# Differential attention's q, k and V by token halves from high and low parts, and three masks of the top-256 search summed on ScalarE

## The chip, the cores and the metric

The kernel runs on one core of a Trainium2 chip. Times are device microseconds (us) of that core from start to end of the program. TensorE is called PE here, VectorE DVE, ScalarE ACT, GpSimd POOL and SyncE SP; PS is PSUM, TensorE's accumulator memory.

## The reference, cut to what matters

```python
S, D, TOPK, Q_BLOCK = 1024, 1024, 256, 128
h = x @ w_in                                    # fp32; columns: a_u a_v b_q b_k b_v c_q c_k c_v i_q i_k i_w
# differential attention: 4 heads, q and k of 2 x 64, v of 128
p = softmax(b_q @ b_k.T / 8 - slope[h] * abs(qpos - kpos)); attn = p[0] - lam * p[1]
out_b = rms_norm(attn @ b_v)
# sparse attention: each query keeps its 256 best keys
score = sum_h i_w[h] * relu(i_q[h] @ i_k.T);  sel = top_k(score, 256)    # block-causal mask
out_c = softmax over sel of c_q @ c_k.T, times c_v
# gMLP mixer
v = layer_norm(gelu(a_v));  out_a = gelu(a_u) * (w_s @ v + b_s)
x = layer_norm(ALPHA * x + concat(out_a, out_b, out_c) @ w_out)          # then FFN, then a second layer
```

The change touches how `b_q`, `b_k` and `b_v` are computed, how the 256 best keys are found, and where the bias `-slope * distance` is made. Nothing after the first layer's attention changes in its own code but for names of semaphores.

## The kernel before

The first layer's input product is done in stages on PE, one weight chunk of 512 KB after another. SP loads the chunks into `ring`, which has four slots; a slot is loaded again once the chunk in it is used (`weights_used`). The order of the stages is the list `ORDER`; the class `Ledger` counts from it which slot, which pair of PSUM banks (four pairs) and which of the three `w_parts` buffers each chunk has. The stages around the change, in PE's order, are: `cqk` and `score` (interleaved), `auv` (gMLP's u and v), `turn_ws`, `bqk` (q and k of differential attention, 8 chunks), `bv` (its V, 4 chunks), `gmlp`, then differential attention itself with `ada` chunks as fill.

`by_feature` (L1296; its products are L1305) does `bqk`: a chunk is 128 output columns, and the product runs over both halves of the 1024 tokens, 16 products of 128x512, with inputs `xT` and `ring` read as plain fp32. `by_token` (L1308; products L1319) does `auv` and `bv`: a chunk is two of the eight 128-row tiles of the weights, for all eight token tiles. The trace records one such fp32 product of 128x512 as two instructions.

Later stages (from `out1` on) do a product in three passes instead. `split_weight` on POOL (L2839) makes of a chunk in `ring` a high part, rounded to fp32r (L2844), and the rest, the low part (L2847), in one of the `w_parts` buffers. The activations are split alike, and PE adds high·high, high·low and low·high. A `w_parts` buffer is free again when PE has used it (`parts_used`).

DVE meanwhile searches the 256th largest score of each query (lines 2250 to 2281). `score` holds the six query blocks 2 to 7, of 384 to 1024 keys. A round fixes one bit of the threshold, 32 rounds in all. In a round the blocks go in two groups of three; for each group two small instructions on three columns work out the next threshold (L2269, L2275), then three counts (L2256) compare a block with its threshold, write the mask as bf16 into `tested` and sum it into `enough`. After the last round come a tail (L2281 to L2298: for each block a mask of ties, a scan that ranks them and three passes that give `mask`), and then the layer norm of gMLP's v (L2307 to L2318), which ends with `v_normed`. PE's `gmlp` (L1477) waits for that. ACT copies results out of PSUM, and POOL has nothing to do while the search runs.

Of the kernel before, what the change touches and what calls it, by code (L numbers as in the profile page):

```python
# [56 lines left out]
def whole(n, dmas=1):  # L57
    return [(dmas, False)] * n
# [5 lines left out]

def sevens(n):
    return [(1, "seven")] * n
# [13 lines left out]

def down_steps(n_k):
    return [(1, "down")] * (7 * n_k)
# [10 lines left out]
    "bqk": (whole(4), [0, 1, 2, 3]),  # L93
    "bv": (whole(4), [None, None, None, 3]),
# [28 lines left out]
         ("bqk", 0), ("bqk", 1), ("bv", 0), ("gmlp", 0), ("ada", 0), ("turn_mix", 0), ("out1", 0), ("turn_mod", 0), ("out1", 1)]  # L123
# [21 lines left out]
class Ledger:  # L145


    def __init__(self):
# [6 lines left out]
        for stage, i in ORDER:  # L155
            chunks, units = STAGES[stage] if stage != "idx" else IDX[i]
            self.pairs_at[stage, i] = list(pairs)
            for c, (dmas, kind) in enumerate(chunks):
                s, q = n_loads % RING, n_halves // 2 % PARTS
# [16 lines left out]
                if kind:  # L176
# [5 lines left out]
                    n_halves += 2  # L182
# [51 lines left out]
def program(nc, t, out):  # L234
    L = Ledger()
    with ExitStack() as ctx:
# [32 lines left out]
        xT = view(0, KT, S)  # L269
# [21 lines left out]
        ranks = view(165.5, S)  # L291
# [7 lines left out]
        dist = view(165.5, S)  # L299
# [126 lines left out]
        dist_made = sem("dist_made")  # L426
        bias_made = sem("bias_made")
        lam_sums = sem("lam_sums")
        lam_exps = sem("lam_exps")
# [4 lines left out]
        norm_var = sem("norm_var")  # L434
        norm_sqrt = sem("norm_sqrt")
        score_added = sem("score_added")
        topk_step, topk_done = sem("topk_step"), sem("topk_done")
# [25 lines left out]
        fl_exp, fl_ln, cum_done = sem("fl_exp"), sem("fl_ln"), sem("cum_done")  # L463
        selw_made, counts_made = sem("selw_made"), sem("counts_made")
        cum_high, cum_split, causal_row_made = sem("cum_high"), sem("cum_split"), sem("causal_row_made")
        pool_w_loaded, pool_w_zeroed = sem("pool_w_loaded"), sem("pool_w_zeroed")
# [664 lines left out]
        def b_bias(u, m):  # L1131
            h, b = heads4[u]
            return bias8[:, h, P * (NB - 1 - b):S], bias_made, 4
# [40 lines left out]
        def after_c(act, u):  # L1174
            rows_c(act, u)
            if u == 4:
                act.wait_ge(norm_var, 2)
                act.activation(o_ssq[:, :], o_ssq[:, :], ACT.Sqrt).then_inc(norm_sqrt, 1)
# [117 lines left out]
        def by_feature(pe, stage, i, source):  # L1296

            for c in range(len(STAGES[stage][0])):
                s, p = L.slot(stage, i, c), L.pair(stage, i, c)
                w = ring[:, s, :].rearrange("p (k n) -> p k n", k=KT)  # L1300
                weights_here(pe, stage, i, c)
                pair_here(pe, stage, i, c)
                for h in HALVES:
                    for k in range(KT):
                        mm = pe.matmul(PS[:, 2 * p + h, :], w[:, k, :], source[:, k, half_of(h)],  # L1305
                                       start=(k == 0), stop=(k == KT - 1))
                mm.then_inc(weights_used[s], 1)

        def by_token(pe, stage, source, width=512):

            for c in range(4):
                s = L.slot(stage, 0, c)
                weights_here(pe, stage, 0, c)
                for k in (2 * c, 2 * c + 1):
                    for b in range(NB):
                        p = L.pair(stage, 0, b // 2)
                        if k == 0 and b % 2 == 0:
                            pair_here(pe, stage, 0, b // 2)
                        mm = pe.matmul(PS[:, 2 * p + b % 2, 0:width], source[:, k, tok(b)],  # L1319
                                       ring[:, s, (k % 2) * width:(k % 2 + 1) * width],  # L1320
                                       start=(k == 0), stop=(k == KT - 1))
                        if k == KT - 1 and b % 2 == 1 and b < NB - 1:
                            mm.then_inc(psum_full[p], 1)
                mm.then_inc(weights_used[s], 1)
# [65 lines left out]
        def _(pe):  # L1390
# [68 lines left out]
            by_token(pe, "auv", xT)  # L1459
# [1690 lines left out]
```

## Time and profile before

| what | value |
|---|---|
| time, median of 3 runs | 2914.8 us (2908.94 to 2917.13) |
| the profiled execution, its own time | 2907.3 us |
| its span | 2905.6 us |
| PE busy | 2804.6 us, 97% of the span |
| DVE, POOL, ACT busy | 1528.2, 1278.1 and 932.2 us |
| PE on the chain of work that ended last | 86% |

The span is the time from the first to the last instruction of the profile. "Busy" counts instructions that run; a DVE or POOL instruction that has been issued and waits inside the engine counts as busy too, so two records of the same form and different lengths tell of a wait. In a timeline, "x2" means two records of one form merged into one line, with the time from the first's start to the second's end.

### The profile page before, as it was taken

The page shows a single profiled execution, that of the slowest core. Times are in us where ns is not written, and L with a number is a line of the kernel's source. Part 1 is how long each engine was busy: PE and PEld are TensorE (multiplying, and loading weights), DVE is VectorE, ACT ScalarE, POOL GpSimd, SP SyncE. Part 2 cuts the span into 40 slices and gives each one's busy share as a digit, 9 for nine tenths or more (in the row PEclk, how much of TensorE's full clock was granted, in tenths as well). Part 3 has the DMA queues.
Part 4 walks back from the last instruction along what each step waited for, and adds up shares of the span by engine and source line. Part 5 has one row for each costly group of instructions (what it writes and reads, how often), then busy time and mean ns, then how long its engine had stood idle before and what let it go on. Part 6 is the DMA issues. An engine that isn't in the chain of part 4 may idle for free.

```text
span 2905.6 us, 33901 instructions
## 1 busy us (share of the span) xinstructions
PE 2804.6 (97%) x12861; PEld 2071.6 (71%) x12861; DVE 1528.2 (53%) x2414; ACT 932.2 (32%) x1590; POOL 1278.1 (44%) x848
## 2 busy tenths in 40 slices
PE   8999999889999999999999999988999899999998
PEld 5444457468888888887778888855466788888886
DVE  0599977656723334243652203556536722235998
ACT  2401036541233332112333200156103344444443
POOL 2000000036777776666677677700126587753020
PEclk9999999999999999999999999999999999999999
DMA  5111137233422223534433333200556333346854
GB/s 114 30 36 37 40 93 195 88 119 119 131 84 87 87 87 116 211 141 168 129 105 116 123 95 97 71 1 1 180 158 197 117 116 108 117 166 220 280 191 172
DMA packets 343393, 344.59 MB, mean 119 GB/s; under 512 B 18368, under 2 KB 261312, under 8 KB 343232
## 3 DMA queue, kind: packets, MB, share of 16 engines
q1 hardware_dynamic: 319424, 275.33, 30.7%
q10 hardware_dynamic: 21328, 59.97, 5.3%
q0 software_dynamic: 2480, 7.13, 1.0%
q8 instruction: 103, 1.69, 0.2%
q14 instruction: 58, 0.48, 0.0%
HBM read 284.61 MB, written 57.77 MB: 118 GB/s over the span
## 4 chain that ended last, share of the span: by engine, by line
PE 86%; DVE 7%; ACT 2%; issue 2%; DMA 1%; ACTq 0%; POOL 0%; SPq 0%; DVEq 0%; POOLq 0%
PE PS L535 25%; PE PS L1355 13%; PE PS L1367 11%; PE PS L851 9%; PE PS L1319 5%; PE PS L1305 4%; PE PS L1598 4%; PE PS L965 3%; PE PS L1436 2%; PE PS L983 2%; PE PS L1003 2%; PE PS L1547 1%; PE PS L1409 1%; PE PS L995 1%; PE PS L1450 1%
## 5 line engine op out<-in xcount | busy, mean ns | idle before, releaser
L2844 POOL TENSOR_SCALAR w_parts<-ring 128x1024 fp32r<-128x1024 f32 x166 | 205.5, 1238 | 802.3 <-DMA ring<-in_w_out 276.7
L594 DVE TENSOR_TENSOR arena<-arena,PS 128x512 f32<-128x512 f32 x266 | 182.9, 687 | 538.6 <-PE PS L535 537.3
L2847 POOL TENSOR_TENSOR w_parts<-ring,w_parts 128x1024 fp32r<-128x1024 f32 x166 | 445.3, 2682 | 13.8
L851 PE MATMUL PS<-w_parts,hid_high 128*128 128x512 f32 x896 | 276.4, 390 | 5.7 <-DVE w_parts L816 4.1
L535 PE MATMUL PS<-tx_high,w_parts 128*128 128x512 f32 x832 | 264.5, 389 | 0.0
L1355 PE MATMUL PS<-hT_high,w_parts 128*128 128x512 f32 x800 | 248.7, 391 | 7.9 <-DVE hT_low L2439 6.5
L1367 PE MATMUL PS<-w_parts,hid_high 128*128 128x512 f32 x704 | 218.3, 391 | 3.9 <-DVE hid_low L636 2.2
L573 POOL TENSOR_TENSOR w_parts<-arena,w_parts 128x512 fp32r<-128x512 f32 x152 | 194.4, 1291 | 44.6 <-ACT w_parts L554 44.5
L573 POOL TENSOR_TENSOR w_parts<-ring,w_parts 128x512 fp32r<-128x512 f32 x114 | 147.3, 1292 | 131.5 <-ACT w_parts L554 131.5
L851 PEld LDWEIGHTS PS<-w_parts,hid_high 128*128 128x128 f32 x896 | 167.7, 188 | 42.6 <-DVE w_parts L816 6.3
L1355 PEld LDWEIGHTS PS<-hT_high,w_parts 128*128 128x128 f32 x800 | 150.4, 188 | 41.1 <-DVE hT_low L2439 8.2
L535 PEld LDWEIGHTS PS<-tx_high,w_parts 128*128 128x128 f32 x832 | 156.2, 188 | 32.3
L851 PE MATMUL PS<-w_parts,hid_low 128*128 128x512 f32 x448 | 174.3, 389 | 0.0
L1073 DVE CUSTOM_DVE_ANT_0 arena<-PS,arena 128x1024 f32<-128x1024 f32 (+7 forms) x160 | 114.8, 755 | 110.7 <-PE PS L971 53.1
L2256 DVE TENSOR_SCALAR_CACHE_REDUCE arena<-arena,misc 128x384 bf16<-128x384 f32 (+2 forms) x192 | 171.4, 942 | 2.2
L535 PE MATMUL PS<-tx_low,w_parts 128*128 128x512 f32 x416 | 161.8, 389 | 0.0
L1355 PE MATMUL PS<-hT_low,w_parts 128*128 128x512 f32 x400 | 155.8, 389 | 0.0
L1367 PEld LDWEIGHTS PS<-w_parts,hid_high 128*128 128x128 f32 x704 | 132.7, 189 | 32.1 <-issue 4.7
L2907 POOL CAST arena<-ident 128x128 bf16<-128x128 f32 x1 | 0.3, 290 | 335.8 <-DVE arena L2298 335.8
L554 ACT CAST w_parts<-arena 128x512 fp32r<-128x512 f32 x152 | 93.7, 618 | 143.0 <-PE PS L535 120.7
L1319 PE MATMUL PS<-ring,arena 128*128 128x512 f32 (+1 forms) x384 | 138.8, 523 | 0.0
L535 PE MATMUL PS<-x1T_high,w_parts 128*128 128x512 f32 x432 | 138.8, 389 | 0.0
(358 smaller groups left out, 5827.6 us busy)
## 6 DMA issues: line engine op xcount, KB each, us to landing
ring<-in_w_in SPq DMA_DIRECT2D x96, 512.0 KB, 3.7
arena<-hid_spill SPq DMA_DIRECT2D x172, 256.0 KB, 3.7
hid_spill<-arena ACTq DMA_DIRECT2D x54, 512.0 KB, 2.9
ring<-in_w_gu SPq DMA_DIRECT2D x52, 512.0 KB, 3.9
ring<-in_w_ada SPq DMA_DIRECT2D x48, 512.0 KB, 5.3
ring<-in_w_ff SPq DMA_DIRECT2D x96, 256.0 KB, 2.9
ring<-in_w_down SPq DMA_DIRECT2D x44, 512.0 KB, 3.7
ring<-in_w_ff SPq DMA_DIRECT2D x40, 512.0 KB, 4.1
```

Source lines behind the costliest of these rows:

```text
L535: mm = pe.matmul(self.product(g, m), w[:, at], x[:, k, :], start=(k == 0 and i == 0), stop=(k == 3 and i == 2))
L573: pool.tensor_tensor(low, self.raw(n), high.bitcast(F32), ALU.subtract).then_inc(self.split_low, 1)
L594: dve.tensor_tensor(out, a, self.product(g, m), ALU.add).then_inc(self.combined, 1)
L851: mm = pe.matmul(PS[:, 4 * (p % 2) + u, :], x, w, start=(j == 0 and i == 0), stop=(j == self.n_k - 1 and i == 2))
L1305: mm = pe.matmul(PS[:, 2 * p + h, :], w[:, k, :], source[:, k, half_of(h)], start=(k == 0), stop=(k == KT - 1))
L1319: mm = pe.matmul(PS[:, 2 * p + b % 2, 0:width], source[:, k, tok(b)], ring[:, s, (k % 2) * width:(k % 2 + 1) * width], start=(k == 0), sto ...
L1355: mm = pe.matmul(PS[:, 2 * p + bank, :], w[:, q, k * P:(k + 1) * P], x[:, k, half_of(h)], start=(k == order[0] and n == 0), stop=(k == ord ...
L1367: mm = pe.matmul(PS[:, 2 * p + half, :], x[:, k, at], w[:, q, half_of(half)], start=(first and n == 0), stop=(last and n == 2))
L1598: mm = pe.matmul(PS[:, 2 * p + 1, :], w[:, k, :], x[:, half_of(h)], start=(k == ks[0]), stop=(k == ks[-1]))
L2256: stepped(dve.tensor_scalar(tested[b], score[b], threshold(column[b]), None, op, ALU.add, accum_out=enough[:, column[b]:column[b] + 1]))
L2844: pool.tensor_scalar(w_high[:, q, :], ring[:, s, :], 1.0, 1.0, ALU.mult, ALU.mult).then_inc(weights_high, 1)
L2847: pool.tensor_tensor(w_low[:, q, :], ring[:, s, :], w_high[:, q, :].bitcast(F32), ALU.subtract).then_inc(weights_used[s], 1)
```

## The change

1. `bqk` and `bv` are done in three passes from high and low parts, and by halves of the tokens. `in_features` and `in_tokens` take the place of `by_feature` and `by_token` there; the order is bqk, bv for tokens 0 to 511, then bqk, bv for tokens 512 to 1023. So each of the 12 chunks is loaded and split twice, 24 chunks of 24 products. Chunks of the new kind `"two"` alternate between the `w_parts` buffers 1 and 2. ACT rounds `xT` (`high_in`), POOL subtracts (`low_in`). For tokens 512 on, the high part is written over the low part of tokens 0 to 511, so that it waits for PE's use of each V chunk of the first half.
2. The search's masks of blocks 7, 6 and 5 (1024, 896, 768 keys) are made without a sum; ACT sums them, by a Square pass over `tested` with accumulation (`sum_masks`). The groups are now (7, 2, 3) and (6, 5, 4). DVE's threshold step of a group waits for ACT's sums of that group (`topk_summed`).
3. ACT's other work is put between the sums, at fixed rounds (`beside_bit`): it is in order, so a copy that waits for PE holds back the next sum, and PE gets a copy no sooner than the round it stands in.
4. In `auv` the last chunk goes token tile by token tile, so that the pairs of banks are full one after another.
5. The distance and bias of differential attention move from the start of the program (POOL, DVE) to behind the search (POOL, and four ACT copies with a scale).

```diff
-    "bqk": (whole(4), [0, 1, 2, 3]),
-    "bv": (whole(4), [None, None, None, 3]),
+    "bqk": (alternate(8), [1, 3, 5, 7]),
+    "bv": (alternate(4), [None, 3]),
...
+            for c in range(8):
+                p, q = L.pair("bqk", h, c // 2), L.part("bqk", h, c)
+                split_here(pe, "bqk", h, c)
+                if c % 2 == 0:
+                    pair_here(pe, "bqk", h, c // 2)
+                for k in range(KT):
+                    if c == 0:
+                        pe.wait_ge(xin_low, KT * h + k + 1)
...
+            def high_in(h, k):
+                for b in range(4 * h, 4 * h + 4) if k == 0 else ():
+                    freed(act, "turn_x", b // 4, b % 4)
+                if h == 1 and k % 2 == 0:
+                    q = L.part("bv", 0, k // 2)
+                    act.wait_ge(parts_used[q], L.part_uses("bv", 0, k // 2) + 1)
+                act.copy(xin(h)[0][:, k, half_of(1 - h)], xT[:, k, half_of(h)]).then_inc(xin_high, 1)
...
+            def beside_bit(i):
+                if i == 0:
+                    copy_cqk(0, 1)
+                if i == 2:
+                    copy_cqk(1, 0)
+                if i == 5:
+                    copy_cqk(1, 1)
+                    act.wait_ge(score_added, len(SCORE_UNITS))
+                if 6 <= i < 14:
+                    high_in(0, i - 6)
+                if 14 <= i < 18:
+                    copy_auv(i - 14)
+                if i == 17:
+                    copy_ws()
+                if i in (18, 20, 23, 25):
+                    copy_tiles("bqk", 0, (18, 20, 23, 25).index(i), bqkT)
+                if 25 <= i < 29:
+                    high_in(1, 2 * (i - 25))
+                    high_in(1, 2 * (i - 25) + 1)
+                if i == 28:
+                    copy_bv(0, 0)
+                    copy_bv(0, 1)
...
                 for b in groups[g]:
-                    stepped(dve.tensor_scalar(tested[b], score[b], threshold(column[b]), None, op, ALU.add,
-                                              accum_out=enough[:, column[b]:column[b] + 1]))
-                counted[g] = steps[0]
+                    if b in ACT_SUMS:
+                        dve.tensor_scalar(tested[b], score[b], threshold(column[b]), None, op).then_inc(topk_masked, 1)
+                        masks[0] += 1
+                    else:
+                        stepped(dve.tensor_scalar(tested[b], score[b], threshold(column[b]), None, op, ALU.add,
+                                                  accum_out=enough[:, column[b]:column[b] + 1]))
...
+            for c in range(2, 8):
+                split_weight("bqk", 0, c)
+            for c in range(3):
+                split_weight("bv", 0, c)
+            low_in(1, 0)
+            low_in(1, 1)
+            split_weight("bv", 0, 3)
```

DVE in a round of the search, before: L2269 and L2275 are the small steps, L2256 the counts.

```order
L2269 TENSOR_SCALAR misc<-misc 128x3
L2275 SCALAR_TENSOR_TENSOR misc<-misc 128x3
L2256 TENSOR_SCALAR arena,misc<-arena,misc 128x384
L2256 TENSOR_SCALAR arena,misc<-arena,misc 128x512
L2256 TENSOR_SCALAR arena,misc<-arena,misc 128x1024
L2269 TENSOR_SCALAR misc<-misc 128x3
L2275 SCALAR_TENSOR_TENSOR misc<-misc 128x3
L2256 TENSOR_SCALAR arena,misc<-arena,misc 128x640
L2256 TENSOR_SCALAR arena,misc<-arena,misc 128x768
L2256 TENSOR_SCALAR arena,misc<-arena,misc 128x896
```

The same round in the changed kernel: L2355 and L2361 are the small steps, L2338 the masks without a sum, L2341 the counts.

```order
L2355 TENSOR_SCALAR misc<-misc 128x3
L2361 SCALAR_TENSOR_TENSOR misc<-misc 128x3
L2338 TENSOR_SCALAR arena<-arena,misc 128x1024
L2341 TENSOR_SCALAR arena,misc<-arena,misc 128x384
L2341 TENSOR_SCALAR arena,misc<-arena,misc 128x512
L2355 TENSOR_SCALAR misc<-misc 128x3
L2361 SCALAR_TENSOR_TENSOR misc<-misc 128x3
L2338 TENSOR_SCALAR arena<-arena,misc 128x896
L2338 TENSOR_SCALAR arena<-arena,misc 128x768
L2341 TENSOR_SCALAR arena,misc<-arena,misc 128x640
```

Two counts have gone from the second group and one from the first; 1024 now stands ahead of its group.

POOL between its small loads at the start and its cast of `ident`, before: nothing stands between the load of `pool_w` and the cast (L2907), which waits for the search; the weights split behind it are those of `out1`.

```order
L2899 MEMSET arena 64x4x64
L2900 MEMSET pool_w 128x256
L2904 DMA pool_w<-in_w_pool 64x64 x4
L2907 CAST arena<-ident 128x128
L2844 TENSOR_SCALAR w_parts<-ring 128x1024
L2847 TENSOR_TENSOR w_parts<-ring,w_parts 128x1024
```

In the changed kernel 24 chunks are split there (L2932 high, L2935 low) and 16 pieces of the activations (L2993); this is the place from the first half's V on.

```order
L2935 TENSOR_TENSOR w_parts<-ring,w_parts 128x1024
L2932 TENSOR_SCALAR w_parts<-ring 128x1024
L2935 TENSOR_TENSOR w_parts<-ring,w_parts 128x1024
L2993 TENSOR_TENSOR xT_r<-xT,xT_r 128x512 x2
L2932 TENSOR_SCALAR w_parts<-ring 128x1024
L2935 TENSOR_TENSOR w_parts<-ring,w_parts 128x1024
L2993 TENSOR_TENSOR xT_r<-xT,xT_r 128x512 x2
L2932 TENSOR_SCALAR w_parts<-ring 128x1024
L2935 TENSOR_TENSOR w_parts<-ring,w_parts 128x1024
L2993 TENSOR_TENSOR xT_r<-xT,xT_r 128x512 x2
L2932 TENSOR_SCALAR w_parts<-ring 128x1024
L2935 TENSOR_TENSOR w_parts<-ring,w_parts 128x1024
```

The last chunk of the first half's V now stands behind the first two pieces of the second half's activations.

ACT between gMLP's copies and the norm's square root, before: one copy of the weights turned (L1779), eight copies of `bqk` (L1663).

```order
L1779 COPY wsT<-PS 128x512
L1663 COPY arena<-PS 128x1024 x8
L1783 ACT_TABLE_LOAD
L1783 ACTIVATE arena<-arena 128x32
L1787 COPY arena<-PS 128x1024 x4
L1790 COPY arena<-misc 128x256
```

In the changed kernel, from the round of index 25 on: L1707 copies `bqk`, L1838 is `high_in`, L1811 the sums.

```order
L1044 ACTIVATE arena,misc<-arena,misc 128x1024 x2
L1303 COPY arena<-PS 128x512
L1305 DMA ada_rows_spill<-arena 4x512
L1058 COPY arena<-PS 128x512
L1044 ACTIVATE arena,misc<-arena,misc 128x128 x2
L1058 COPY arena<-PS 128x512 x2
L1044 ACTIVATE arena,misc<-arena,misc 128x896 x2
L1058 COPY arena<-PS 128x128
L1044 ACTIVATE arena,misc<-arena,misc 128x256 x2
L1303 COPY arena<-PS 128x512
L1305 DMA ada_rows_spill<-arena 4x512
L1058 COPY arena<-PS 128x512
```

Each pair of L1838 now stands behind three sums of a round of the search.

## Rows read from the trace of the kernel before

**Rows 1.** Windows: busy us (instructions) per engine, PEclk, DMA share, GB/s.
```profile
150.80:346.60 195.80, 195.80 (x461) 86.93 (x460) 191.34 (x521) 16.12 (x20) 0.00 (x0) 1.00 0.13 38
```

**Rows 2.** Chain of work in order of time: start us, us, what.
```profile
237.18 109.87 PE PS L1305 x256
347.05 54.93 PE PS L1319 x128
401.98 3.43 PE PS L1477 x8
```

**Rows 3.** Timeline of DVE: search begins, one round, its tail begins (start us, us).
```profile
150.31 0.48 DVE L2242 MEMSET arena<- 64x64 f32 x6
...
161.69 0.16 DVE L2269 TENSOR_SCALAR misc<-misc 128x3 int32<-128x3 f32 x1
161.88 0.16 DVE L2275 SCALAR_TENSOR_TENSOR misc<-misc 128x3 int32<-128x3 int32 x1
...
163.29 1.27 DVE L2256 TENSOR_SCALAR_CACHE_REDUCE arena<-arena,misc 128x1024 bf16<-128x1024 f32 x1
...
167.69 0.17 DVE L2269 TENSOR_SCALAR misc<-misc 128x3 int32<-128x3 f32 x1
...
347.80 0.17 DVE L2281 TENSOR_SCALAR misc<-misc 128x6 f32<-128x6 f32 x1
```

**Rows 4.** Timeline of DVE, end of the search's tail and first norm step.
```profile
363.98 0.68 DVE L2286 TENSOR_SCALAR arena<-arena,misc 128x896 bf16<-128x896 f32 x1
...
369.67 0.75 DVE L2286 TENSOR_SCALAR arena<-arena,misc 128x1024 bf16<-128x1024 f32 x1
...
376.03 2.28 DVE L2307 TENSOR_REDUCE arena<-arena 128x32 f32<-128x2048 f32 x1
```

**Rows 5.** Timeline of DVE, last step of the gMLP norm.
```profile
391.05 2.29 DVE L2318 TENSOR_TENSOR arena<-arena 128x2048 f32<-128x2048 f32 x1
```

**Rows 6.** Chain of the whole span, a stage from high and low parts.
```profile
626.63 43.79 PE PS L1367 x192
```

**Rows 7.** Timeline of POOL in that stage: one weight chunk.
```profile
637.97 1.05 POOL L2844 TENSOR_SCALAR w_parts<-ring 128x1024 fp32r<-128x1024 f32 x1 [1.91 <-PE PS L1367]
639.10 2.38 POOL L2847 TENSOR_TENSOR w_parts<-ring,w_parts 128x1024 fp32r<-128x1024 f32 x1
```

**Rows 8.** One source line of POOL, 128x512: duration ns min/median/max.
```profile
L573 POOL TENSOR_TENSOR w_parts<-arena,w_parts x152: 1280/1288/1312, 808.7 to 2566.9; 128x512 fp32r<-128x512 f32 x152
```

**Rows 9.** Timeline of DVE around 1436 us, POOL splitting beside it.
```profile
1436.17 5.34 DVE L2397 TENSOR_TENSOR arena<-arena 128x1024 f32<-128x1024 f32 x2
1443.14 1.90 DVE L2480 TENSOR_SCALAR misc<-misc 128x4 f32<-128x4 f32 x1 [1.63 <-ACTq L1719]
```

**Rows 10.** Timeline of POOL in the same stretch.
```profile
1436.05 1.05 POOL L2844 TENSOR_SCALAR w_parts<-ring 128x1024 fp32r<-128x1024 f32 x1 [1.00 <-PE PS L1355]
1437.18 3.25 POOL L2847 TENSOR_TENSOR w_parts<-ring,w_parts 128x1024 fp32r<-128x1024 f32 x1
...
1442.62 2.39 POOL L2847 TENSOR_TENSOR w_parts<-ring,w_parts 128x1024 fp32r<-128x1024 f32 x1
```

**Rows 11.** Timeline of DVE around 1778 us.
```profile
1778.17 1.43 DVE L2640 TENSOR_SCALAR arena<-arena,misc 128x1024 f32<-128x1024 f32 x1
1779.63 4.62 DVE L2643 SCALAR_TENSOR_TENSOR arena<-arena,misc 128x1023 f32<-128x1023 f32 x2
```

**Rows 12.** Timeline of POOL in the same stretch.
```profile
1777.76 1.30 POOL L2844 TENSOR_SCALAR w_parts<-ring 128x1024 fp32r<-128x1024 f32 x1 [0.71 <-PE PS L1355]
1779.14 2.71 POOL L2847 TENSOR_TENSOR w_parts<-ring,w_parts 128x1024 fp32r<-128x1024 f32 x1
```

**Rows 13.** Timeline of ACT: a copy from PSUM, an accumulating pass.
```profile
250.95 1.01 ACT L1663 COPY arena<-PS 128x1024 f32<-128x1024 f32 x1 [12.61 <-PE PS L1305]
...
410.58 1.15 ACT L1033 ACTIVATE arena<-arena,misc 128x1024 f32<-128x1024 f32 x1 [5.95 <-DVE misc L1073]
```

**Rows 14.** DMA issues, from the page: KB each, median us from issue to landing.
```profile
ring<-in_w_in SPq DMA_DIRECT2D x96, 512.0 KB, 3.7
```

More of the change, by code:

```diff
@@ L1294, in rows_out, with by_token @@
             act.dma_start(ada_dram[:, 512 * g:512 * (g + 1)], ada_row[0:P:32, g % 2, :]).then_inc(ada_stored, 16)
[L1296 to L1309, printed above, removed]
+        def by_token(pe, stage, source, width=512, by_tile=False):
             for c in range(4):
@@ L1313, in by_token @@
                 weights_here(pe, stage, 0, c)
-                for k in (2 * c, 2 * c + 1):
[L1315 to L1322, printed above, removed]
+                steps = ([(k, b) for b in range(NB) for k in (2 * c, 2 * c + 1)] if by_tile and c == 3 else
+                         [(k, b) for k in (2 * c, 2 * c + 1) for b in range(NB)])
@@ new lines, in by_token @@
+                for k, b in steps:
+                    p = L.pair(stage, 0, b // 2)
+                    if k == 0 and b % 2 == 0:
+                        pair_here(pe, stage, 0, b // 2)
+                    mm = pe.matmul(PS[:, 2 * p + b % 2, 0:width], source[:, k, tok(b)],
+                                   ring[:, s, (k % 2) * width:(k % 2 + 1) * width],
+                                   start=(k == 0), stop=(k == KT - 1))
+                    if k == KT - 1 and b % 2 == 1 and b < NB - 1:
+                        mm.then_inc(psum_full[p], 1)
@@ new lines, in _ @@
+            for k in range(KT):
+                if k % 2 == 0 and k < 6:
+                    s = L.slot("auv", 0, k // 2)
+                    pool.wait_ge(weights_used[s], L.slot_uses("auv", 0, k // 2) + 1)
+                if k == 6:
+                    unit_here(pool, "auv", 0, 1)
+                low_in(0, k)
+            for c in range(2, 8):
+                split_weight("bqk", 0, c)
+            for c in range(3):
+                split_weight("bv", 0, c)
+            low_in(1, 0)
+            low_in(1, 1)
@@ new lines, in _ @@
+            split_weight("bv", 0, 3)
+            low_in(1, 2)
+            low_in(1, 3)
+            split_weight("bqk", 1, 0)
+            low_in(1, 4)
+            low_in(1, 5)
+            split_weight("bqk", 1, 1)
+            low_in(1, 6)
+            low_in(1, 7)
+            for c in range(2, 8):
+                split_weight("bqk", 1, c)
+            for c in range(4):
+                split_weight("bv", 1, c)
+            pool.wait_ge(topk_done, NB - 2)
+            pool.iota(dist, pattern=[[-1, S]], base=S - P, channel_multiplier=1,
+                      allow_small_or_imprecise_dtypes=True).then_inc(dist_made, 1)
@@ new lines, in _ @@
+            pool.iota(behind, pattern=[[1, P]], base=0, channel_multiplier=-1,
+                      allow_small_or_imprecise_dtypes=True).then_inc(dist_made, 1)
+            pool.wait_ge(dist_made, 2)
+            for part in (dist[:, S - P:S], behind):
+                pool.tensor_scalar(part, part, 0.0, None, ALU.max).then_inc(dist_made, 1)
+            pool.wait_ge(dist_made, 4)
+            pool.tensor_tensor(dist[:, S - P:S], dist[:, S - P:S], behind, ALU.add).then_inc(dist_made, 1)
+            for h in range(4):
+                pool.wait_ge(dist_made, 5 + h + 1)
+                pool.memset(bias8[0:64, h, S - 64:S], NEG).then_inc(bias_made, 1)
```

180 lines of the change are left out of this document (113 added, 67 removed).

## The prediction

> **What bounds the kernel now.** I read the windows first, then the chain of waits, then DVE's timeline, and last the places where POOL splits weights beside DVE. While the search runs, PE is busy for all of 195.8 us and DVE for 191.3, and POOL for nothing [rows 1]. The chain runs through PE alone: 109.87 us of `bqk`, 54.93 of `bv`, then `gmlp` at 401.98 [rows 2]. DVE ends its norm at 391.05 + 2.29 = 393.3 [rows 5]. So PE is the bound here and DVE has 8.7 us to spare. What PE gives up beyond that is gained only if DVE's chain (search, tail, norm) becomes shorter too. `gmlp` needs `v_normed`, and attention follows it; this stage is therefore settled by one number, the time at which `gmlp` can start, now 402.0.
>
> **PE's products.** Before: 109.87 + 54.93 = 164.8 us [rows 2]. After: 24 chunks of 24 passes, 576 of them. 192 such passes take 43.79 us [rows 6], so a chunk takes 5.47 and all take 131.4. PE alone would be 33.4 us shorter, and `gmlp` could start at 368.6.
>
> **DVE's rounds with nothing beside them.** A round is 167.69 - 161.69 = 6.00 us [rows 3]. The count of 1024 keys has a record of 1.27 us, of which about 0.07 lies under the next. A mask of the same form without a sum stands in the tail, 0.75 us for 1024 keys and 0.68 for 896 [rows 4], with a like overlap. So 1024 keys go from 1.20 to 0.67, and by the same slopes 896 from 1.07 to 0.60 and 768 from 0.93 to 0.53. That takes off 1.40 and a round is 4.6 us. The search took 347.7 - 150.8 = 197 [rows 3]; 33 passes over the blocks make it 46 us shorter. The tail to 376.0 is 28.3 us, the norm to 393.3 is 17.3 [rows 3 to 5]; neither changes.
>
> **ACT's sums.** An accumulating pass over 1024 elements is 1.15 us [rows 13]; with 896 and 768 in proportion about 3.1 us a round, under DVE's 4.6. A copy from PSUM beside it is 1.01 [rows 13], and a round still fits. ACT comes free for PE only in its fixed rounds, though: that is where delays of DVE reach PE.
>
> **POOL's splits, beside the search for the first time.** A chunk takes POOL 1.05 + 2.38 us and a gap of 0.08, 3.5 us of PE's 5.47 [rows 7], so POOL keeps pace if left alone. The 16 low passes over 128x512 are 1.29 each [rows 8]. What these do to DVE is the term that decides. At 1443.14 a DVE instruction on four columns takes 1.90 us and ends at 1445.04; POOL's subtraction beside it runs from 1442.62 to 1445.01 [rows 9, 10]. At 1778.17 a DVE pass with one SBUF input and no sum, the form of the masks, takes 1.43 us instead of 0.75 and ends 0.54 after POOL's pass (1777.76 + 1.30) [rows 11, 12]. POOL's next subtraction then takes 2.71 instead of 2.38, since it waits for that pass. Two DVE additions with two SBUF inputs, some 2.4 us of work, take 5.34 while POOL splits one chunk, and POOL's subtraction takes 3.25 [rows 9, 10]. I read this as one port that either engine holds for a whole instruction, and that goes to the other in between. It is met by DVE instructions with two SBUF inputs and by plain tensor-scalar ones.
>
> In a round these are the two small steps of each group and the three masks, seven instructions; the three counts left (some 2.0 us) can run beside POOL if they don't need the port. No row shows a count beside POOL. The form is slower for 1024 keys (1.27 against 0.75) [rows 3, 4], so I take it as free of the port; were it not, the result is in the fourth case below. The Trainium skill (SBUF — State Buffer, Who interferes with whom) says that a `tensor_scalar` which also writes out its accumulator does not enter the modes that take the shared ports. By that rule the counts are free and the sum stays; without it `gmlp` would be some 7 us later. No run shown here tells.
>
> **How a round goes beside splits.** Take DVE released by the end of a subtraction. Mask and counts last about 1.9 us, the two small steps 0.4. POOL's next rounding starts 1.9 us after the last subtraction's end (the idle time in [rows 7]), so DVE's second small step meets it and waits up to 1.0, and the mask behind it meets the subtraction and waits about 2.3. Then the same state is there again, one chunk later. So half a round costs one chunk, and a round 2 x 5.47 = 10.9 us instead of 4.6. It is the pattern of the two additions per chunk in [rows 9].
>
> **The stage walked through.**
> - `auv` is as long as `bv` (54.93) and ends with `turn_ws` at 237.18 [rows 2]; it begins at about 181.8, and its first of four chunks ends at 195.5. Only then can the first new chunk be loaded, which takes 3.7 us [rows 14]. So the rounds of index 0 to 8 pass at 4.6 (the last ends at 196).
> - From 199 to 240 POOL has two splits and eight low passes, 17 us on the port. I let DVE lose somewhat over half of it, 10 us: round 17 ends at 248 instead of 238. PE's first chunk needs a copy in round 15 and starts some 4 us late, at about 242.
> - Rounds 18 to 21 run beside splits at 10.9 each, to about 291.
> - POOL then stands, in order, before the first two low passes of the second half. These wait for ACT's `high_in` in round 25, and the split of the last V chunk is behind them. PE has used what was split by 242 + 11 x 5.47 = 302 and waits. Rounds 22 to 25 are undisturbed and end at about 312; ACT's pass, two low passes and a split put PE back at 321. PE loses 19 us.
> - The second half's last pieces stand in round 28, again beside splits, at about 339: PE loses some 11 us more. PE's end is then 321 + 13 x 5.47 + 11 = 403, about as before.
> - Rounds 29 to 31 end at about 365. In the tail nearly every instruction has two SBUF inputs or is a plain tensor-scalar one. Until POOL is done (398) two or three get through per chunk; I take 46 us instead of 28.3, to 411. The norm is undisturbed: 411.3 + 17.3 = 428.6.
>
> `gmlp` starts at 428.6 instead of 402.0, 26.6 us later. ACT's bv and bias copies (4 x some 1.0, after the square root at 421) and the table load end at about 429 and are hidden behind that wait; the moved iota and distance work of POOL (about 3 us from 411) lie there too. If DVE were on time they would end some 8 us behind PE, which is also when ACT's first exponential was due before (410.58 [rows 13] against `gmlp` at 401.98). Taking the bias from DVE's start gives nothing, as DVE idles there.
>
> **The sum.** The profiled execution took 2907.3 us. 2907.3 + 26.6 = 2933.9. The median of the runs shown is 7.5 us above it (2914.8), so I forecast 2941.4 us.
>
> **The rivals.**
> - *Port as above* (forecast): 2941, with 2930 to 2955 for the phase of the two engines. For it: the three places in [rows 9 to 12], one of them four columns wide, as the search's small steps nearly are. Against it: in all of them POOL and DVE met in other stages, never in the search.
> - *No meeting that matters* (the other side): masks that write bf16, or steps on three columns, slip past POOL. Then rounds stay at 4.6, ACT's copies wait for PE rather than the reverse, DVE's norm ends at about 350 to 363, and PE is the bound at 368.6 plus some 3.8 at the start of the second half, where ACT and POOL must follow PE's last V chunk: 372.4, 29.6 us earlier. 2914.8 - 29.6 = 2885. It decides where v_normed comes before 402; for that DVE may lose at most some 38 us to POOL, whose time on the port is 24 x 3.43 + 16 x 1.29 = 103 us. The tail and masks alone make that hard.
> - *Half of it*: either the masks or the small steps are free. A round beside splits is then some 7 to 8 us, round 31 ends at about 336, PE loses 8 to 10 us, the norm ends at 400 to 404. Time 2912 to 2917, no change.
> - *Counts too*: every DVE pass of a round takes the port. PE's first chunk is another 4 us late and the second half's start 3 more, v_normed at 436: 2949. With ACT's sums late as well it could reach 2965.
>
> **How the numbers follow.** Chances: port as above 0.62, counts too or worse 0.08, half of it 0.11, no meeting 0.19. The time is that of the first, 2941. The range runs from 2886 to 2962, so that it takes in the half case and the way between the cases, and leaves out most of the no-meeting case and the worst. The first case's own range is 2930 to 2955. About 0.3% (8.7 us) is what a measurement of this kernel can tell from no change. Faster by more: 0.19 and a little of the half case, 0.21. Within: 0.10. Slower by more: 0.69.
>
> **What would show it.** In the changed kernel's trace: (1) chunks of 24 passes at 5.47 us wherever PE doesn't wait; (2) rounds of 4.6 us before 199 us and of about 11 us from 248 to 290, with masks and small steps of 2 to 3 us and counts of unchanged length; (3) a wait of PE of some 19 us before the last V chunk of the first half; (4) a tail of about 46 us, and PE waiting for DVE before `gmlp` until about 429. Masks of 0.75 us beside splits would make the prediction wrong, as would `gmlp` before 402.

## The result, and the profile of the changed kernel

| | before | changed |
|---|---|---|
| time, median | 2912.8 us (4 runs, 2908.9 to 2917.1) | 2933.9 us (4 runs, 2932.9 to 2936.0) |
| profiled execution, its span | 2907.3, 2905.6 us | 2933.6, 2931.4 us |
| `gmlp` starts | 401.98 [rows 2] | 421.98 |
| attention's first product starts | 407.09 | 429.92 |

The ratio of the times is 1.0073 with an interval of 1.0055 to 1.0090, so the change makes the kernel slower. Of the 25.8 us by which the span grew, 22.8 stand at attention's first product.

Windows of the changed kernel, columns as in [rows 1]:

```profile
150.80:346.60 195.80, 171.61 (x545) 106.37 (x544) 191.48 (x413) 117.51 (x226) 75.09 (x47) 0.93 0.22 60
354.00:404.40 50.40, 46.16 (x204) 37.92 (x202) 49.28 (x34) 6.07 (x7) 28.41 (x15) 0.99 0.29 84
```

The first line is the stretch of [rows 1]. PE is no longer busy throughout (171.6 of 195.8 us), and DVE still is. DVE's busy time is the same as before although three sums a round are gone from it. POOL, idle before, is busy for 75.1 us. The second line holds the end of the search's last round and its tail. The tail's first instruction (L2368, on six columns) starts at 356.66 and the norm's first at 404.43, so the tail takes 47.8 us; before it took 28.2 [rows 3, 4].

What PE waits for between 230 and 425 us (instruction, what was waited for, us in total, times, longest):

```profile
PE PS L1516 <- issue: 21.8, 1, 21.8
PE PS L1358 <- POOL w_parts L2935: 11.8, 1, 11.8
PE PS L1339 <- POOL xT_r L2993: 7.6, 3, 6.1
PE PS L1339 <- issue: 3.1, 1, 3.1
PE PS L1339 <- POOL w_parts L2935: 1.1, 1, 1.1
```

L1516 is `gmlp`. It waits for 21.8 us; the profile names nobody for it, and the chain shows whom: it comes down DVE's search, tail (to 404.4) and norm. The others are, in this order, the last V chunk of the first half, the inputs of the second half's first chunk, the first chunk of all, and one more chunk. Without them PE would be done over 20 us earlier, and `gmlp` would start no sooner.

The wait of 11.8 us goes through ACT. In these rows of ACT, POOL and PE, ACT's rounding of the second half's inputs stands behind its sums and copies of a round, POOL's low passes wait for it, and the split that PE needs is behind them:

```profile
308.23 1.14 ACT L1838 CAST xT_r<-xT 128x512 fp32r<-128x512 f32 x2
...
308.92 2.48 POOL L2993 TENSOR_TENSOR xT_r<-xT,xT_r 128x512 fp32r<-128x512 f32 x2 [12.47 <-ACT xT_r L1838]
311.37 1.04 POOL L2932 TENSOR_SCALAR w_parts<-ring 128x1024 fp32r<-128x1024 f32 x1
312.49 2.59 POOL L2935 TENSOR_TENSOR w_parts<-ring,w_parts 128x1024 fp32r<-128x1024 f32 x1
...
315.14 0.80 PE L1358 MATMUL PS<-w_parts,bqkT_r 128*128 128x512 f32 x1 [11.77 <-POOL w_parts L2935]
```

The list of ACT's instructions given for the changed kernel in the section on the change (L1044, L1058, L1303) is not this place. Those are attention's, from about 433 us on.

The DVE instructions from 150 to 404 us by shape (busy us, mean ns of one). L2338 are the masks without a sum, L2341 the counts, L2355 and L2361 the small steps:

```profile
L2338 DVE TENSOR_SCALAR arena<-arena,misc 128x1024 bf16<-128x1024 f32 x32 | 37.4, 1168 | 1.1
L2338 DVE TENSOR_SCALAR arena<-arena,misc 128x768 bf16<-128x768 f32 x32 | 33.3, 1041 | 0.0
L2341 DVE TENSOR_SCALAR_CACHE_REDUCE arena<-arena,misc 128x640 bf16<-128x640 f32 x32 | 27.9, 872 | 0.0
L2355 DVE TENSOR_SCALAR misc<-misc 128x3 int32<-128x3 f32 x64 | 21.0, 328 | 0.0
L2341 DVE TENSOR_SCALAR_CACHE_REDUCE arena<-arena,misc 128x384 bf16<-128x384 f32 x32 | 19.4, 606 | 0.0
L2361 DVE SCALAR_TENSOR_TENSOR misc<-misc 128x3 int32<-128x3 int32 x62 | 16.9, 272 | 2.1
```

And the counts of the kernel before, with its small step:

```profile
L2256 DVE TENSOR_SCALAR_CACHE_REDUCE arena<-arena,misc 128x640 bf16<-128x640 f32 x32 | 28.1, 878 | 1.1
L2256 DVE TENSOR_SCALAR_CACHE_REDUCE arena<-arena,misc 128x384 bf16<-128x384 f32 x32 | 19.6, 611 | 1.1
L2269 DVE TENSOR_SCALAR misc<-misc 128x3 int32<-128x3 f32 x64 | 10.5, 163 | 0.0
```

The counts didn't change (872 against 878 ns). The masks are 1168 and 1041 ns in the mean, where one with nothing beside it is 750 and 610. The small steps take 328 and 272 ns in the mean, where either took 163 before. So two of the three kinds of instruction meet something, and the counts do not.

What they meet is seen in DVE's timeline around 270 us (start, us):

```profile
265.34 0.75 DVE L2338 TENSOR_SCALAR arena<-arena,misc 128x1024 bf16<-128x1024 f32 x1
...
267.21 2.29 DVE L2355 TENSOR_SCALAR misc<-misc 128x3 int32<-128x3 f32 x1
269.53 0.16 DVE L2361 SCALAR_TENSOR_TENSOR misc<-misc 128x3 int32<-128x3 int32 x1
269.73 1.22 DVE L2338 TENSOR_SCALAR arena<-arena,misc 128x896 bf16<-128x896 f32 x2
270.86 0.87 DVE L2341 TENSOR_SCALAR_CACHE_REDUCE arena<-arena,misc 128x640 bf16<-128x640 f32 x1
...
272.23 2.78 DVE L2338 TENSOR_SCALAR arena<-arena,misc 128x1024 bf16<-128x1024 f32 x1
...
276.52 4.03 DVE L2338 TENSOR_SCALAR arena<-arena,misc 128x896 bf16<-128x896 f32 x2
280.47 0.87 DVE L2341 TENSOR_SCALAR_CACHE_REDUCE arena<-arena,misc 128x640 bf16<-128x640 f32 x1
```

POOL in the same stretch, splitting weights (L2932 rounds, L2935 subtracts):

```profile
265.48 1.52 POOL L2932 TENSOR_SCALAR w_parts<-ring 128x1024 fp32r<-128x1024 f32 x1 [1.67 <-PE PS L1342]
267.09 2.39 POOL L2935 TENSOR_TENSOR w_parts<-ring,w_parts 128x1024 fp32r<-128x1024 f32 x1
270.92 1.05 POOL L2932 TENSOR_SCALAR w_parts<-ring 128x1024 fp32r<-128x1024 f32 x1 [1.45 <-PE PS L1342]
272.06 2.40 POOL L2935 TENSOR_TENSOR w_parts<-ring,w_parts 128x1024 fp32r<-128x1024 f32 x1
276.36 1.05 POOL L2932 TENSOR_SCALAR w_parts<-ring 128x1024 fp32r<-128x1024 f32 x1 [1.91 <-PE PS L1342]
277.49 2.64 POOL L2935 TENSOR_TENSOR w_parts<-ring,w_parts 128x1024 fp32r<-128x1024 f32 x1
```

The step on three columns that starts at 267.21 ends at 269.50, just behind POOL's subtraction (267.09 + 2.39 = 269.48). It has 0.16 us of work. The mask at 272.23 ends 0.55 us after the subtraction that ends at 274.46. The two masks at 276.52 meet the rounding and then the subtraction and take 4.03 instead of 1.22. The count at 270.86 runs beside the rounding (270.92 to 271.97) for its usual 0.87. This is the port of the prediction. The Trainium skill (SBUF — State Buffer, Who interferes with whom) says that a `tensor_scalar` which also writes out its accumulator does not enter the modes that take the shared ports. The rows agree: 0.87 us beside POOL, and 0.88 in the kernel before.

`gmlp` and attention's first products in the changed kernel:

```profile
421.98 6.26 PE L1516 MATMUL PS<-arena,wsT 128*128 128x512 f32 x8 [21.82 <-issue]
429.92 1.99 PE L976 MATMUL PS<-arena 64*128 64x512 f32 x8 [1.68 <-issue]
```

`gmlp` itself takes 6.26 us against 3.43 [rows 2]. The granted clock is 0.5, that is 1.2 GHz, from 403.3 on, after PE went idle at 400.

### The profile page after: what moved, and what is told of

It reads as the page before. It is cut to its first block, busy times and chain, and to the rows that moved or that the text cites. A ratio compares the mean times of both kernels' runs of the same rounds, so it can differ in the third digit from the quotient of the medians.

```text
span 2931.4 us, 34570 instructions
## 1 busy us (share of the span) xinstructions
PE 2784.9 (95%) x13046; PEld 2115.4 (72%) x13053; DVE 1552.5 (53%) x2306; ACT 1041.4 (36%) x1808; POOL 1393.4 (48%) x920
## 4 chain that ended last, share of the span: by engine, by line
PE 77%; DVE 15%; issue 5%; ACT 2%; DMA 1%; ACTq 0%; POOL 0%; DVEq 0%; SPq 0%; POOLq 0%
PE PS L546 25%; PE PS L1394 13%; PE PS L1406 11%; PE PS L862 9%; PE PS L1637 4%; PE PS L976 3%; DVE arena L2341 2%; PE PS L994 2%; PE PS L1014 2%; DVE arena L2338 2%; PE PS L1586 1%; PE PS L1448 1%; PE PS L1006 1%; PE PS L1318 1%; PE PS L1489 1%
## 5 line engine op out<-in xcount | busy, mean ns | idle before, releaser
L2932 POOL TENSOR_SCALAR w_parts<-ring 128x1024 fp32r<-128x1024 f32 x190 | 236.2, 1243 | 1000.7 <-DMA ring<-in_w_out 279.4
L2935 POOL TENSOR_TENSOR w_parts<-ring,w_parts 128x1024 fp32r<-128x1024 f32 x190 | 504.2, 2654 | 15.9
L862 PE MATMUL PS<-w_parts,hid_low 128*128 128x512 f32 x448 | 174.3, 389 | 0.0
L976 PE MATMUL PS<-arena 64*128 64x512 f32 (+2 forms) x480 | 119.9, 528 | 18.6 <-DVE misc L1084 15.6
L1406 PE MATMUL PS<-w_parts,hid_low 128*128 128x512 f32 x352 | 137.5, 391 | 0.0
L1044 ACT ACTIVATE arena<-arena,misc 128x1024 f32<-128x1024 f32 (+7 forms) x160 | 123.1, 776 | 26.5 <-DVE misc L1084 26.0
```

What stands on the lines that cost most here:

```text
L862: mm = pe.matmul(PS[:, 4 * (p % 2) + u, :], x, w, start=(j == 0 and i == 0), stop=(j == self.n_k - 1 and i == 2))
L976: mm = pe.matmul(PS[:, 2 * m + c // 512, 0:w], self.q(j, m, b), self.k(j, m, c, w), start=True, stop=more[m] is None)
L1044: act.activation(p, p, ACT.Exp, bias=rowmin[:, n % 8:n % 8 + 1], scale=-1.0, accum_out=expsum[:, n % 8:n % 8 + 1]).then_inc(self.probs_mad ...
L1406: mm = pe.matmul(PS[:, 2 * p + half, :], x[:, k, at], w[:, q, half_of(half)], start=(first and n == 0), stop=(last and n == 2))
L2932: pool.tensor_scalar(w_high[:, q, :], ring[:, s, :], 1.0, 1.0, ALU.mult, ALU.mult).then_inc(weights_high, 1)
L2935: pool.tensor_tensor(w_low[:, q, :], ring[:, s, :], w_high[:, q, :].bitcast(F32), ALU.subtract).then_inc(weights_used[s], 1)
```

## The experiments

All ratios are against the kernel before, measured beside it. My theory was the one on record: POOL's splits and DVE's plain instructions exclude each other, and DVE, made late by that, holds `gmlp`. Rivals were that ACT's work in fixed rounds is the cause, that the sums on ACT are, or that the low clock after PE's waits is.

**1. The splits made small.** POOL splits 16 of 1024 columns from the third chunk on; the rest of the parts is stale, so q, k and V are not those of the reference.

```diff
-                pool.tensor_scalar(w_high[:, q, :], ring[:, s, :], 1.0, 1.0, ALU.mult, ALU.mult
+                n = 16 if stage in ("bqk", "bv") and (stage, i, c) not in (("bqk", 0, 0), ("bqk", 0, 1)) else 1024
+                pool.tensor_scalar(w_high[:, q, 0:n], ring[:, s, 0:n], 1.0, 1.0, ALU.mult, ALU.mult
...
+                pool.tensor_tensor(w_low[:, q, 0:n], ring[:, s, 0:n], w_high[:, q, 0:n].bitcast(F32),
...
```

> The changed kernel, but from the third weight chunk of bqk on POOL splits 16 of the 1024 columns of a chunk (the rest of the parts keeps the numbers of the first two chunks, so q, k and V of differential attention are wrong). All instructions, waits and PE's passes stay; only POOL's time on the port goes (22 x 3.43 us less some 0.3 each). Port theory: rounds of 4.6 us from 240 us on except where ACT waits for PE, no wait of PE before the last V chunk of the first half, the tail some 28 to 30 us, the norm's end before PE's, gmlp at about 370 to 378; time 2880 to 2888. Rival, the sums on ACT and PE's copies in fixed rounds cost the time by themselves: gmlp stays above 410 and the time above 2922.

Measured: 2887.2 us, ratio 0.992 (0.990 to 0.994). Of the search's rounds behind 250 us about half are 4.6 or 4.7 and the others 5.3 to 9.0. Its tail starts at 325.1 (356.7 in the changed kernel) and takes 28.4 us (47.8), the norm is done at 370.9 and `gmlp` starts at 374.9. DVE by shape, and PE's only wait before `gmlp` of over 1 us:

```profile
L2338 DVE TENSOR_SCALAR arena<-arena,misc 128x1024 bf16<-128x1024 f32 x32 | 27.1, 845 | 1.1
L2355 DVE TENSOR_SCALAR misc<-misc 128x3 int32<-128x3 f32 x64 | 13.2, 206 | 5.9 <-ACT arena L1811 5.9
...
PE PS L1339 <- issue: 3.1, 1, 3.1
```

So 51 us of DVE's delay and both of PE's long waits hang on what POOL splits. With ACT's sums, ACT's fixed rounds, the order and the number of PE's passes left as they are, the kernel would be 47 us faster than the changed one. ACT's fixed rounds alone cost nothing of this size.

**2. The splits in pieces.** The same work of POOL, with the rounding in two instructions and the subtraction in four:

```diff
+PIECES = (2, 4)
...
+                for j in range(n_low):
+                    cols = slice(j * 1024 // n_low, (j + 1) * 1024 // n_low)
+                    ins = pool.tensor_tensor(w_low[:, q, cols], ring[:, s, cols], w_high[:, q, cols].bitcast(F32),
+                                             ALU.subtract)
```

> The changed kernel with POOL's rounding of a chunk in 2 pieces of 512 columns and its subtraction in 4 of 256, the result the same. POOL's total time on the port grows by some 8%, but a DVE instruction waits for a piece (0.7 us) and not for 2.4. Port theory with a whole instruction held: a round beside splits about 6.5 us instead of 8 to 9, the norm ends at about 395, PE some 402; time 2908 to 2918, 16 to 26 us below the changed kernel. Rival, what counts is POOL's total time on the port: no change or slower, 2932 to 2940.

Measured: 2918.9 us, ratio 1.0028 (1.0015 to 1.0040), 15 us better than the changed kernel and 0.9 above the range expected. DVE's mask and PE's waits:

```profile
L2339 DVE TENSOR_SCALAR arena<-arena,misc 128x1024 bf16<-128x1024 f32 x32 | 30.4, 948 | 1.1
...
PE PS L1359 <- POOL w_parts L2941: 15.5, 4, 8.1
PE PS L1340 <- POOL w_parts L2941: 5.5, 4, 3.4
PE PS L1340 <- POOL xT_r L3000: 4.1, 1, 4.1
```

A DVE instruction now waits for a piece and not for a whole pass (the mask takes 948 instead of 1168 ns), and the tail begins at 341 and ends at 379. But POOL waits more in turn, its chunks come later, and PE now waits 25.1 us for them (20.5 in the changed kernel). PE ends at 408.3, 6 us later than expected, and is the bound again; the norm is done at 399.1. Beside the waits it is the clock that holds PE up: in the stretches at 1.2 GHz that follow waits it is busy for 20.9 us (14.9 in the changed kernel). What DVE wins, PE partly loses.

**3. ACT's sums alone**, put into the kernel before, with everything else plain and POOL idle:

```diff
+TOPK_GROUPS = ((7, 2, 3), (6, 5, 4))
+ACT_SUMS = (5, 6, 7)
...
+                    if b in ACT_SUMS:
+                        dve.tensor_scalar(tested[b], score[b], threshold(column[b]), None, op).then_inc(topk_masked, 1)
```

> The kernel before with the second part of the change alone: three masks without a sum, ACT sums them, ACT's copies put into fixed rounds. POOL splits nothing beside the search. Port theory: rounds of 4.6 us throughout, the norm ends at 345 to 350 while PE goes on to 402, time as before within 3 us. Rival, ACT's sums bound the rounds: rounds of 5 us or more without any split beside them, and copies late for PE, time above 2918.

Measured: 2910.6 us, ratio 1.0006 (0.9995 to 1.0016), no change. A round takes 4.6 us, but for that of index 17 (6.2), and the search is over at 304.7 instead of 347.8 [rows 3]. The norm ends at 358.3 and not at 345 to 350, since DVE waits 8.3 us for ACT's square root, which stands behind copies of `bqk`. `gmlp` still starts at 403.2, since PE is the bound. So this half of the change does what it says, brings 43 us on the search, and gains nothing by itself.

**4. The splits alone**: the changed kernel with all sums left on DVE.

```diff
-ACT_SUMS = (5, 6, 7)
+ACT_SUMS = ()
```

> The changed kernel with all six counts and sums on DVE again (ACT sums nothing, so its copies follow PE alone). Port theory: only the four small steps of a round and the tail meet POOL; rounds start at 6.0 us and go to 8 to 10 beside splits, PE runs through to about 371 and waits for DVE until 425 to 437; time 2935 to 2950. Rival, PE's loss comes from ACT's fixed rounds: with these gone the norm would end at about 394 and the time would be 2900 to 2908.

Measured: 2949.4 us, ratio 1.0134 (1.0113 to 1.0154), at the upper end of the range expected. `gmlp` starts at 436.9, the search's tail at 391.1 instead of 347.8, and the tail takes 28.2 us, as POOL is done by then. DVE by shape, and PE's wait for it:

```profile
L2355 DVE TENSOR_SCALAR misc<-misc 128x3 int32<-128x3 f32 x64 | 45.6, 713 | 0.0
L2341 DVE TENSOR_SCALAR_CACHE_REDUCE arena<-arena,misc 128x1024 bf16<-128x1024 f32 x32 | 40.9, 1279 | 1.1
...
PE PS L1516 <- issue: 65.8, 1, 65.8
```

All six counts keep their length (1279 ns for 1024 keys, 1274 before) although POOL splits beside them. The whole loss falls on the small steps: the first takes 713 ns in the mean and the second (L2361) 295, both instead of 163, which is 43.4 us, all of the 43.3 by which the search grew. It is the cleanest evidence on the counts, and it ends the case "counts too". The long waits of PE for POOL's parts are nearly gone (2.8 us are left), since ACT, without sums, is bound to no round of DVE. In experiment 1, with ACT's fixed rounds and hardly any splits, they are gone too: PE's long waits need both. But they don't set the time: PE is done at 371, stands for 65.8 us, and the kernel is 15.5 us slower than the changed one.

**5. V first and plain**, then q and k by halves from high and low parts: 16 chunks split instead of 24.

```diff
-         ("bqk", 0), ("bv", 0), ("bqk", 1), ("bv", 1), ("gmlp", 0), ...
+         ("bv", 0), ("bqk", 0), ("bqk", 1), ("gmlp", 0), ...
```

> The changed kernel with V done first, in plain fp32 and undivided as before (4 chunks, 54.9 us), then q and k by halves from high and low parts (16 chunks split, not 24). Splits of whole chunks now begin near 292 us, when the search is nearly done at 4.6 us a round. Port theory: search ends at about 310, the tail is stretched to 50 us and the norm by some 8, so v_normed at 380 to 390; PE ends at 384 to 388; gmlp at 385 to 392 and time 2895 to 2904, below both kernels. Rival, the loss is PE's own (three passes by halves, waits at the change of halves) and not the search's: gmlp no earlier than 402 and time 2912 or more.

Measured: 2914.6 us, ratio 1.0009 (0.9999 to 1.0018), no change: the expectation was 10 us or more too low, and both marks of the rival came (`gmlp` at 402 or later, 2912 us or more).

**6.** The same with the splits in pieces as in experiment 2:

> The same as the kernel with V first, and POOL's passes of a chunk in 2 and 4 pieces. Port theory: DVE's tail is stretched less (to about 38 us), PE is the bound and may wait for POOL where DVE's passes come between the pieces (some 8 us); time within 5 us of the kernel with whole passes, 2893 to 2905. Rival, pieces always help: below 2893.

Measured: 2922.9 us, ratio 1.0032 (1.0020 to 1.0044), so it missed too. V first puts the splits beside the end of the search, the tail and the norm. In 5 the tail begins at 323.1 (expected 310) and takes 54.8 us, and DVE then waits 7.4 us for ACT's square root, so that its norm ends at 405.3. PE starts `gmlp` at 405.7 without a wait. Before that it waited 4.7 + 4.6 + 4.5 us, and it was busy for some 18 us in two stretches at 1.2 GHz (298.5 to 303.7 and 351.5 to 368.5). So both engines were some 20 us later than expected and came out together: the rival's PE loss is real, and so is DVE's. In 6, PE waits for POOL's parts for 18.3 us and starts `gmlp` at 410.8; the tail takes 42.3 us. Its norm is drawn out to 50.8 us, which looks like the port and is not. These are a DVE and an ACT row of it:

```profile
401.31 0.35 DVE L2405 RECIPROCAL arena<-arena 128x32 f32<-128x32 f32 x1 [32.19 <-ACT arena L1874]
...
398.72 1.02 ACT L1710 COPY arena<-PS 128x1024 f32<-128x1024 f32 x1 [9.86 <-PE PS L1343]
...
401.05 0.23 ACT L1874 ACTIVATE arena<-arena 128x32 f32<-128x32 f32 x1
```

DVE is idle for 32 us. The square root (L1874) stands on ACT behind copies that wait for PE; I had put it there. In 6 it costs nothing, since PE is as late. What 5 and 6 show is that 16 splits instead of 24 didn't bring the time below that of before when they met the tail, and that pieces didn't help where PE was as late as DVE.

**7. PE kept busy through its wait**: 90 products into a free bank between the last V chunk and the wait for the norm, results unused.

```diff
+            pair_here(pe, "gmlp", 0, 0)
+            for _ in range(90):
+                pe.matmul(PS[:, 2 * L.pair("gmlp", 0, 0), :], w_high[:, 1, 0:P], xT_r[:, 0, 0:512], start=True, stop=True)
             pe.wait_ge(v_normed, 1)
```

> The changed kernel with 90 extra passes of 128x512 on PE (results thrown away, about 20.4 us) between the end of V and the wait for the norm, where PE stands idle for 21.8 us at the lower clock. If the granted clock after the wait costs time, gmlp's eight products take 3.4 us and not 6.3 and attention's first products run at the full clock: time 3 to 6 us below the changed kernel, 2928 to 2931. Rival, attention waits for DVE and ACT anyway and the clock costs nothing beyond gmlp: 2931 to 2934.

Measured: 2931.9 us, ratio 1.0062 (1.0045 to 1.0078), 2.0 us under the changed kernel's median. That lies in the rival's range. The intervals of the two ratios overlap, so the times alone don't show a gain; the trace does.

```profile
422.25 3.70 PE L1519 MATMUL PS<-arena,wsT 128*128 128x512 f32 x8 [1.53 <-DVE arena L2408]
427.62 1.99 PE L976 MATMUL PS<-arena 64*128 64x512 f32 x8 [1.68 <-issue]
```

`gmlp` runs at the full clock and attention starts 2.3 us earlier. Its first eight products take 1.99 us in both kernels. So the low clock behind the last wait costs some 2 to 3 us. The releaser is now named, too: DVE's last norm step.

**8. One half from parts.** What the runs so far say together: ACT's sums leave DVE some 40 us, and POOL's splits take more than that. Against experiment 3 the changed kernel's search ends 51.9 us later and its tail takes 19.5 us more, so most of the loss falls in the rounds. So only tokens 0 to 511 are done from high and low parts (12 chunks), and tokens 512 to 1023 in plain fp32 behind them.

```diff
+            for c in range(8) if h == 1 else ():
...
+                    mm = pe.matmul(PS[:, 2 * p + c % 2, :], ring[:, s, k * P:(k + 1) * P], xT[:, k, half_of(1)],
+                                   start=(k == 0), stop=(k == KT - 1))
...
-                if 25 <= i < 29:
-                    high_in(1, 2 * (i - 25))
-                    high_in(1, 2 * (i - 25) + 1)
```

> Only tokens 0 to 511 are done from high and low parts (12 chunks of 24 passes); tokens 512 to 1023 are done in plain fp32 as before the change (12 half chunks of 16 instructions, half of 109.87 + 54.93 = 82.4 us together). ACT's high parts and POOL's low parts of the second half are gone, and POOL splits nothing after some 300 us. Port theory: the rounds up to there go as in the changed kernel (round 24 ends near 302), those behind at 4.6, so that the search ends at about 336, the tail takes 28.5 us as it did with small splits and the norm 17.3, done by about 382. PE: first new chunk at 240.5, 12 x 5.47 = 66 to 306, then 82.4 us to 389 without a wait. gmlp at 389 to 391 with PE at the full clock, 11 to 13 us before the kernel before; 2898 to 2903, faster by 0.3 to 0.45%. Rival (the tail is long in the changed kernel for another reason than POOL's splits, say ACT's late sums or memory traffic): the tail stays near 50 us, v_normed comes after 400, and the time is that of the kernel before or worse.

Measured: 2900.7 us (6 runs), ratio 0.9963 (0.9950 to 0.9976). It beats both kernels. POOL does nothing between 308 and 354 us. The search's tail starts at 338.8 and takes 28.2 us, and PE goes from one product to the next into `gmlp`:

```profile
308.00:354.00 46.00, 46.00 (x113) 21.25 (x112) 43.89 (x106) 25.43 (x48) 0.00 (x0) 1.00 0.23 64
...
367.04 2.28 DVE L2415 TENSOR_REDUCE arena<-arena 128x32 f32<-128x2048 f32 x1
...
382.19 2.29 DVE L2426 TENSOR_TENSOR arena<-arena 128x2048 f32<-128x2048 f32 x1
...
389.65 3.17 PE L1367 MATMUL PS<-ring,xT 128*128 128x512 f32 x7
392.66 3.60 PE L1540 MATMUL PS<-arena,wsT 128*128 128x512 f32 x8
```

The norm is done at 384.5, 8 us before PE needs it. `gmlp` came forward by 402.0 - 392.8 = 9.2 us, and the medians differ by 10.0 (2910.7 and 2900.7). `gmlp` is 2 to 4 us later than expected: the first chunk started at 242.0 and not at 240.5, and the 12 chunks took 68.4 us instead of 65.6, with some 6 us at 1.2 GHz at their start. The rival's long tail is gone with the splits beside it. This run has fewer splits and has them earlier, both at once, and the number seems to count for more than the place. Against experiment 3, in which POOL splits nothing, the tail ends later by 34.1 us with 12 chunks split (here), by 44.9 with 16 (experiment 5, most of them beside the tail) and by 71.5 with 24 (the changed kernel). That is 2.8, 2.8 and 3.0 us per chunk, its low passes included.

## Why the prediction was right, step by step

The sign, the cause and the place were right, and the chosen case is the one that came, within its own range (2930 to 2955). The range around all cases, 2886 to 2962, took in "no change" and most of the others, so a time inside it says little. `gmlp` is 20.0 us later where 26.6 were forecast. The median rose by 21.1 us against the runs beside it.

- **PE's products**: right. A chunk of 24 passes takes 5.44 us (three in 16.3 us) where PE runs at the full clock; forecast 5.47.
- **Rounds alone**: right, 4.6 us from 153.7 on.
- **What takes the port**: right in all three kinds, masks and small steps yes, counts no. Experiment 4 settled the last, which no row of before told.
- **Rounds 9 to 17**: 247.4 for the end, forecast 248. PE's first chunk started at 240.6 after a wait of 3.1; forecast about 242 after some 4.
- **A round beside splits**: mis-sized, 10.9 forecast. From the round of index 20 on they take 6.7 and 9.6 us in turn, 16.3 for two, which is three chunks for four half rounds where I had one for each. The step that failed is "so DVE's second small step meets it and waits". I had let 1.9 us of masks and counts follow each subtraction. The second group has only one count, and after the subtraction that held its last mask (277.49 + 2.64) DVE needs 0.87 for the count and 0.36 for the steps. Its next mask then begins just before POOL's next rounding, as at 265.34 against 265.48, and it is POOL that waits (1.52 instead of 1.05). That half round, 265.0 to 267.2, is free of waits, and so is every fourth. Rounds 18 to 21 ended at 281.3 and not at 291.
- **Rounds 22 to 25**: forecast undisturbed, 21 us. They took 25.5, since PE's V chunks and POOL's splits ran on into them, and ended at 306.8 (forecast 312). The last V chunk's wait was there, but 11.8 us instead of 19. The second half's start cost 7.6 (forecast 11). PE was done at about 400 (403), and that nearness is luck: waits 10.6 us shorter than forecast were in the main made up for by the clock (see below).
- **Rounds 26 to 31 and the tail**: the rounds took 49.9 us (forecast 53), so the tail began at 356.7 where 365 was forecast. It took 47.8 us (forecast 46), and ended at 404.4 against 411. Three to four instructions got through per chunk, not two or three, but the tail had more of POOL's work beside it, as it began earlier.
- **The norm**: right, 17.5 us (forecast 17.3); one pass took 2.43 instead of 2.29 us.
- **Left out of the sum**: the clock after each of PE's waits. `gmlp` ran at 1.2 GHz, 6.26 instead of 3.43 us, which makes the gap 22.8 at attention's first product. Ahead of it PE was busy for 14.9 us at 1.2 GHz, in three stretches that each follow a wait (from 240.6, 315.1 and 335.9). That is some 7.5 us of PE's time, an estimate from half the speed. It didn't show in the time because DVE was later.
- **From the profiled run to the median**: I added 7.5 us because the profiled run of before was that much under the median shown. Other runs of before beside the experiments had medians from 2910.7 to 2912.8, and the changed kernel's profiled run (2933.6) is at its median (2933.9). So the 7.5 us were a scatter of before, and nearly all of the gap between 2941 and 2934. That the sum without them, 2933.9, is the time measured is luck: 6.6 us too many at `gmlp` are nearly made up for by 2.8 us of clock and 3.0 us behind attention's first product, and neither was in the sum.

How 22.8 became 25.8 over the rest of the span isn't settled. The stage of [rows 6] starts 24.1 us later than before, and what is left lies within what single executions differ by.

## What to carry to other kernels

Before an idle engine is given work, look at what its instructions share with its neighbours', not at how idle it is. Here PE's shorter products (33 us) and DVE's shorter search (43 us) were both real, and POOL's 103 us of work on a shared port undid both. Ask what one piece of the shared work takes from the neighbour (here some 3 us of DVE for each chunk split), and give the idle engine only as many pieces as leave the neighbour on time: half of the change, with 12 chunks split, was 10 us faster than the kernel before where all of it, with 24, was 21 us slower.

## What the runs showed of the hardware that I had not expected

- A small instruction can pay as much at the port as a large one. A step on three columns with 0.16 us of work takes 2.29 us at 267.21, and a mask of 1024 with 0.75 us of work takes 2.78 at 272.23: each waits for some 2 us.
- A pass over 1024 keys with a sum is longer alone than one without (1.27 against 0.75 us), but it stays as long when POOL splits: 1.28 us in the mean of experiment 4, where a mask without a sum takes up to 2.78 in the changed kernel.
- Pieces shift the loss from the engine that waits to the one that splits: DVE's mask fell from 1168 to 948 ns, and PE's waits for POOL rose from 20.5 to 25.1 us.
